# Row maxima of the mLSTM gates turned into columns: a masked sum on VectorE in place of sixteen one-row products on TensorE

## The chip, the cores and the metric

One core of a Trainium2 chip runs the whole kernel in one launch. The metric is device time in microseconds, from the first to the last instruction of the program as the device reports it; several runs are made and their median is given.

## What is computed

A trunk of two pre-norm residual layers over 256 frames of width 1024. Layer 0 mixes by pooling and forgetting attention and ends in a dense SwiGLU; layer 1 mixes by stick-breaking attention (8 heads of 64) and mLSTM (4 heads of 128) and ends in a top-2-of-8 expert SwiGLU. The change lies in the mLSTM of layer 1. Cut to that:

```python
log_i, log_f = gate_chunks(i_pre), log_sigmoid(gate_chunks(f_pre))
bcum = jnp.cumsum(log_f, axis=-1)
log_d = bcum[..., :, None] - bcum[..., None, :] + log_i[..., None, :]
m_out = jnp.maximum(inter, jnp.max(jnp.where(tri, log_d, -jnp.inf), axis=-1))
d_mat = jnp.exp(log_d - m_out[..., None])
num, den = ..., ...
h = num / jnp.maximum(jnp.abs(den), jnp.exp(-m_out))[..., None]
```

For each head and frame the kernel needs the running maximum in two layouts. As a row (frames along the free axis, the same row on all 128 partitions) it goes into the exponents of d_mat; as a column (frames along the partitions) it goes into exp(-m_out), the floor of the denominator.

## The kernel before

The matrices are multiplied as sums of three products of a high and a low part. A weight piece of 128x2048 lands in `raw` (six slots), ACT writes its high part (`make_high`, L674), DVE its low part (`make_low`, L679, "the subtraction"), and PE multiplies (L881 to L883). There are three buffers for the parts, so step n of the odd mixer splits piece n+3.

The odd mixer is a loop over 14 steps, `ODD_JOBS`, that each engine walks in its own program, in an order written out by hand. In step n PE first projects job n (`project`: 48 products, some 6 us), and then does the small products that the tables put into step n. The tables near the change are `SB_SCORES = {3: 0, 5: 2, 8: 4, 10: 6}` (scores of a pair of stick-breaking heads, L1210 and L1213), `SB_LATER = {4: 0, 6: 2, 9: 4, 11: 6}` (L1222 to L1224), `SB_VALUES = {5: 0, 7: 2, 10: 4, 12: 6}` (weights times values, L1003 and L1005), `ROWS_TURNED_AT = 8`, `SILU_AT = 9` and `ML_EXPONENTS_AT = 11`.

One pair of stick-breaking heads goes round the engines, here heads 4 and 5:

- PE writes scores at the end of step 8 (L1210, L1213); ACT takes abs, exp and log of them (L1678, L1679, L1682); DVE makes two parts per head (L2156, L2158); POOL masks the first part (L1849).
- At the end of step 9 PE sums it over later keys (L1222 to L1224); DVE subtracts that (L2168); ACT takes the exponential (L1688); POOL masks it (L1849); PE multiplies it with the values at the end of step 10 (L1003).

The row maxima are made in steps 2 and 3 (`gate_rows`, a scan on DVE) as `ml_r`, 128 x (4 heads x 256 frames), each row repeated on all partitions. In step 8, after its projection, PE turns them (`rows_to_columns`, L1197): 8 fp32 products of a 1x128 row with a 1x1 one, which the trace shows as 16 instructions, give 8 columns in bank 3, two tiles by four heads. DVE subtracts the column of sums from the bank (L2224) into `m_em`, at the end of its own step 8, behind the parts of heads 4 and 5 and a chunk of the convolution (L2139, L2142), and ahead of the subtraction of piece 11. ACT takes the exponential of `m_em` in step 11 (L1721); DVE reads it in step 12 (L2192). Bank 3 is next filled in step 9, by the sum of head 5 (L1222, the second of its pair).

Of the kernel before, what the change touches and what calls it, by code (L numbers as in the profile page):

```python
# [30 lines left out]
ALU = mybir.AluOpType  # L31
# [3 lines left out]
P = 128  # L35
# [10 lines left out]
ML_H = 4  # L46
# [229 lines left out]
def plan_banks():  # L276
    banks = Banks()

    def norm(j):
        for i in range(4):  # L280
            banks.fill(("norm", j, i), i)

    norm(0)
    banks.fill("vectors", 2)
    banks.fill("fgate_rows", 5)
    banks.fill("fgate", 4)
    for n in range(EVEN_STEPS):
        if n < len(EVEN_JOBS):
            banks.fill(("even", n), 6 + n % 2)
        if n == EVEN_SUMS_AFTER:  # L290
            banks.fill("frows", 3)
        if n in FOX_SCORES:
            for i in range(2):
                banks.fill(("fox_s", FOX_SCORES[n] + i), i)
        if n in FOX_TURNS:
            for i in range(2):
                banks.fill(("fox_pt", FOX_TURNS[n] + i), 2)
        if n in FOX_VALUES:
            banks.fill(("fox_o", FOX_VALUES[n] // 2), 3, 2)
        for g2 in range(2):  # L300
            if n == POOL_AT:
                banks.fill(("pool", g2), 4 + g2)
            if n == POOL_AT + 1:
                banks.fill(("poolmix", g2), 4 + g2)
    for t in range(T):
        for nh in range(2):
            banks.fill(("wout", 0, 2 * t + nh), 6 - 2 * t + nh)
    norm(1)
    for c in range(NCH):
        for j in range(4):  # L310
            banks.fill(("g", c, j), j % 2)
            banks.fill(("u", c, j), 2 + j % 2)
    for n in range(4):
        banks.fill(("fdown", n), 4 + n)
    norm(2)
    banks.fill("mgate_rows", 5)
    banks.fill("mgate", 4)
    for n in range(len(ODD_JOBS)):
        banks.fill(("odd", n), 6 + n % 2)
        if n == ODD_SUMS_AFTER:  # L320
            banks.fill("mcum", 2)
        if n in ODD_ROWS_AFTER:
            for h in ODD_ROWS_AFTER[n]:
                banks.fill(("mrow", h), 4 + h % 2)
        for i in range(2):
            if n in SB_SCORES:
                banks.fill(("sb_z", SB_SCORES[n] + i), i)
            if n in SB_LATER:
                banks.fill(("sb_lat", SB_LATER[n] + i), 2 + i)
        if n in SB_VALUES:  # L330
            banks.fill(("sb_o", SB_VALUES[n] // 2), 4 + SB_VALUES[n] // 2 % 2, 2)
        if n == ROWS_TURNED_AT:
            banks.fill("mr", 3)
        for i in range(2):
            if n in ML_SCORES:
                banks.fill(("ml_s", ML_SCORES[n] + i), i)
            if n in ML_VALUES:
                banks.fill(("ml_n", ML_VALUES[n] + i), 2 + i)
    for n in range(4):
        banks.fill(("wout", 1, n), 4 + n)  # L340
    for h in range(ML_H):
        banks.fill(("ml_t", h), h % 2)
    for t in range(T):
        for half in range(2):
            banks.fill(("xt", t, half), 2 * t + half)
    for t in range(T):
        banks.fill(("rparts", t), 5 - t, NQ)
    banks.fill("router", 6)
    banks.fill("rank", 5)
    banks.fill("counts", 7)  # L350
    for k in range(DK):
        banks.fill(("gather", 0, k), NG + k % NG)
    for k in range(DK):
        banks.fill(("gather", 1, k), 6 + k % 2)
    before = list(banks.count), list(banks.signals)
    banks.fill("sgt", 7)
    for part in range(len(PARTS)):
        for r in range(NG):
            banks.fill(("mg", part, r), r, NQ)
            banks.fill(("mu", part, r), NG + r, NQ)  # L360
    for r in range(NG):
        banks.fill(("md", r), DOWN_BANKS[r], NQ)
    for q in range(NQ):
        banks.fill(("mc", q), NG + q)
    per_item = [[a - b for a, b in zip(*pair)] for pair in zip((banks.count, banks.signals), before)]
    return banks.uses, *per_item


def build_trunk(nc, x_d, w, cst_d, out_d):
    uses, bank_fills_per_item, bank_signals_per_item = plan_banks()  # L370

    with ExitStack() as ctx:
# [3 lines left out]
        def sem(name):  # L376
            return ctx.enter_context(nc.semaphore(name))
# [12 lines left out]
        def ps(use):  # L390
            return bank[uses[use][0]][:, :]
# [198 lines left out]
        conv_silu = sem("conv_silu")  # L590
        mr_ready = sem("mr_ready")
        mem_ready = sem("mem_ready")
        sbl_ready = sem("sbl_ready")
        sbsp_ready = sem("sbsp_ready")
        sbsp_masked = sem("sbsp_masked")
# [263 lines left out]
        def _(pe):  # L859
# [328 lines left out]
                    last = mm(ps(use)[:, SEQ + t * P:SEQ + (t + 1) * P], li[t], ident, start=True, stop=True)  # L1188
                last.then_inc(fill_sem(use), 1)

            def rows_to_columns():

                open_bank(pe, "mr")
                pe.wait_ge(mr_ready, ML_H)
                for t in range(T):
                    for h in range(ML_H):
                        last = mm(ps("mr")[:, t * ML_H + h:t * ML_H + h + 1], ml_r[0:1, h, t * P:(t + 1) * P],  # L1197
                                  ones[0:1, 0:1], start=True, stop=True)
                last.then_inc(fill_sem("mr"), 1)

            def stick_scores(g):

                pair = (g, g + 1)
# [53 lines left out]
            for n in range(len(ODD_JOBS)):  # L1257
                if n:
                    project("odd", n, ODD_JOBS, N_ODD)
                else:  # L1260
                    first_odd_half(1)
                    small_columns("mgate", 2 * ML_H)
                if n == ODD_SUMS_AFTER:
                    pe.wait_ge(mlf_ready, 1)
                    prefix_sums("mcum", ml_lf, ML_H)
                for h in ODD_ROWS_AFTER.get(n, ()):
                    gate_rows(h)
                if n in SB_LATER:
                    for i in range(2):
                        stick_later(SB_LATER[n] + i)  # L1270
                if n == ROWS_TURNED_AT:
                    rows_to_columns()
                if n in SB_SCORES:
                    stick_scores(SB_SCORES[n])
                if n in SB_VALUES:
                    stick_values(SB_VALUES[n])
                for i in range(2):
                    if n in ML_VALUES:
                        ml_values(ML_VALUES[n] + i)
                    if n in ML_SCORES:  # L1280
                        ml_scores(ML_SCORES[n] + i)
# [222 lines left out]
        def _(act):  # L1504
# [193 lines left out]
            for n in range(len(ODD_JOBS)):  # L1698
                if n not in DVE_ODD_JOBS:
                    act.wait_ge(*filled(("odd", n)))  # L1700
                    dst, scale, shape = job_target(ODD_JOBS[n])
                    func = ACT.Sigmoid if ODD_JOBS[n][1] == "mo" else ACT.Copy
                    fn(dst, shape(ps(("odd", n))), func, scale=scale).then_inc(drain_sem(("odd", n)), 1)
                if n + 1 == min(SB_SCORES):
                    fn(unread[:, :], inv_ms[:, 2, :], ACT.Exp)
                if n in SB_SCORES:
                    stick_logs(SB_SCORES[n])
                if n in SB_VALUES:
                    mix_high_part(SB_VALUES[n] // 2, ("sb_o", SB_VALUES[n] // 2))
                high_parts(N_ODD + n + SPLITS)  # L1710
                if n in SB_LATER:
                    stick_weights(SB_LATER[n])
                if n == SILU_AT:

                    act.wait_ge(conv_ready, 8)
                    for half in range(2):
                        v = mqk[:, 4 * half:4 * half + 4, :]
                        fn(v, v, ACT.Silu).then_inc(conv_silu, 1)
                if n == ML_EXPONENTS_AT:
                    act.wait_ge(*drained("mr"))  # L1720
                    fn(m_em, m_em, ACT.Exp).then_inc(mem_ready, 1)  # L1721
                    for h in range(ML_H):
                        act.wait_ge(me_in, h + 1)
                        fn(ml_e[h], ml_e[h], ACT.Exp).then_inc(me_ready, 1)
                if n == len(ODD_JOBS) - 1:
                    fn(unread[:, :], inv_ms[:, 2, :], ACT.Sqrt)
                for i in range(2):
                    if n in ML_VALUES:
                        ml_squares(ML_VALUES[n] + i)
# [140 lines left out]
        def _(dve):  # L1870
# [328 lines left out]
            for n in range(len(ODD_JOBS)):  # L2199
# [20 lines left out]
                    if n in CONV_AT:  # L2220
                        conv_chunk(2 * CONV_AT[n] + 1)
                if n == ROWS_TURNED_AT:
                    dve.wait_ge(*filled("mr"))
                    V.tensor_tensor(m_em, ps("mr")[:, 0:T * ML_H].rearrange("p (t h) -> p t h", t=T), m_rn_f,  # L2224
                                    ALU.subtract).then_inc(drain_sem("mr"), 1)
                if n == ML_EXPONENTS_AT:
                    for h in range(ML_H):
                        ml_exponent(h)
# [293 lines left out]
```

## Time and profile before

| | |
|---|---|
| runs | 1427.05, 1425.03, 1422.69 us; median 1425.03 us |
| the profiled execution | span 1422.2 us; the page gives no other time for it |
| PE busy | 1394.8 us of 1422.2 (98%) |
| DVE, ACT, POOL busy | 441.0, 328.8 and 29.7 us |
| the odd mixer's steps 7 to 11 | from about 421 us to 461 us of the span |

The times are medians over whole executions; the profile is of one execution, and every time inside the kernel is counted from the start of its span. A row of a timeline gives the start, the length, the engine and the line; in brackets stands how long the engine had been idle before it and what released it. PEclk is the share of the full TensorE clock that was granted.

### The profile page before, as it was taken

The numbers are of one execution on the slowest core, as the hardware profiler recorded it, in microseconds if no ns is written. First come the engines' busy times: TensorE is split into PE (matmuls) and PEld (weight loads), VectorE is DVE, ScalarE is ACT, GpSimd is POOL, SyncE is SP. The second block draws the span as 40 slices with busy tenths as digits, with TensorE's granted clock in tenths as the row PEclk, the third lists the DMA queues.
The fourth block names the chain that finished last, engine by engine and source line by source line (L and its number), as shares of the span: only waits on it lengthen the run. The fifth ranks groups of instructions, "written<-read, shape, count | busy, mean of one in ns | idle before, by whom it ended". The sixth has DMA issues, their size and how long they took to land.

```text
span 1422.2 us, 33237 instructions
## 1 busy us (share of the span) xinstructions
PE 1394.8 (98%) x15137; PEld 833.4 (59%) x15137; DVE 441.0 (31%) x748; ACT 328.8 (23%) x528; POOL 29.7 (2%) x42
## 2 busy tenths in 40 slices
PE   6999999999999999999999999999999999999997
PEld 6987888888899853453453353353354354344344
DVE  4656655655686742101101101101101101101102
ACT  4645545445566531000000000000000000000001
POOL 2000000000012100000000000000000000000000
PEclk9999999999999999999999999999999999999998
DMA  9734555556443489999999999999999999999980
GB/s 296 252 119 146 195 177 194 191 180 198 149 120 140 148 332 326 401 419 389 391 418 387 392 417 389 394 415 393 388 414 400 392 405 402 393 402 408 393 332 32
DMA packets 133041, 438.42 MB, mean 308 GB/s; under 512 B 10690, under 2 KB 64160, under 8 KB 116512
## 3 DMA queue, kind: packets, MB, share of 16 engines
q1 hardware_dynamic: 131824, 433.26, 80.1%
q0 software_dynamic: 1072, 2.98, 0.7%
q8 instruction: 121, 1.98, 0.6%
q14 instruction: 24, 0.20, 0.0%
HBM read 435.16 MB, written 1.05 MB: 307 GB/s over the span
## 4 chain that ended last, share of the span: by engine, by line
PE 95%; DVE 3%; DMA 1%; issue 0%; ACT 0%; POOL 0%; SPq 0%; DVEq 0%
PE bank L1366 41%; PE bank L1387 20%; PE bank L1131 6%; PE bank L881 6%; PE bank L883 6%; PE bank L882 6%; PE bank L1132 4%; PE bank L1134 1%; PE bank L1415 1%; PE bank L1435 1%; DMA raw<-in_ev_w_in 1%; DVE arena L2142 0%; PE bank L1003 0%; PE bank L1049 0%; POOL arena L1849 0%
## 5 line engine op out<-in xcount | busy, mean ns | idle before, releaser
L1366 PE MATMUL bank<-ring,arena 128*32 128x512 f32 (+1 forms) x6144 | 583.5, 540 | 0.0
L1366 PEld LDWEIGHTS bank<-ring,arena 128*32 128x32 f32 x6144 | 197.7, 110 | 365.2 <-issue 362.5
L1387 PE MATMUL bank<-ring,arena 128*32 128x256 f32 x5376 | 291.5, 379 | 0.0
L1387 PEld LDWEIGHTS bank<-ring,arena 128*32 128x32 f32 x5376 | 175.1, 110 | 116.7 <-issue 3.1
L679 DVE TENSOR_TENSOR low<-raw,high 128x2048 fp32r<-128x2048 f32 x73 | 167.3, 2294 | 85.1 <-ACT high L674 84.9
L674 ACT ACTIVATE high<-raw 128x2048 fp32r<-128x2048 f32 x73 | 139.3, 1910 | 55.8 <-PE bank L883 44.1
L1131 PE MATMUL bank<-ht_both,high 128*128 128x512 f32 x392 | 140.5, 398 | 0.6 <-DVE ht_both L1901 0.6
L2413 DVE TENSOR_TENSOR expert_rows<-expert_rows,bank 128x512 f32<-128x512 f32 (+1 forms) x48 | 29.8, 621 | 344.3 <-issue 217.3
L1788 ACT ACTIVATE expert_rows<-bank 128x512 f32<-128x512 f32 (+1 forms) x48 | 25.9, 544 | 422.9 <-PE bank L1366 422.9
L1132 PE MATMUL bank<-ht_both,low 128*128 128x256 f32 x448 | 116.8, 281 | 0.0
L1799 ACT ACTIVATE y_h<-bank 128x256 fp32r<-128x256 f32 x24 | 9.2, 383 | 403.9 <-PE bank L1387 403.9
L2425 DVE TENSOR_TENSOR y_l<-bank,y_h 128x256 fp32r<-128x256 f32 x24 | 10.2, 425 | 270.5 <-ACT y_h L1799 270.5
L1132 PEld LDWEIGHTS bank<-ht_both,low 128*128 128x128 f32 x448 | 84.7, 189 | 5.1
L1131 PEld LDWEIGHTS bank<-ht_both,high 128*128 128x128 f32 x392 | 73.8, 188 | 16.1 <-issue 0.8
L881 PE MATMUL bank<-ht_both,high 128*128 128x256 f32 x224 | 65.9, 294 | 2.4 <-DVE ht_both L1901 1.8
L883 PE MATMUL bank<-ht_both,low 128*128 128x256 f32 x224 | 64.7, 289 | 0.0
L882 PE MATMUL bank<-ht_both,high 128*128 128x256 f32 x224 | 64.7, 289 | 0.0
L881 PE MATMUL bank<-high,ht_both 128*128 128x256 f32 x160 | 47.0, 294 | 0.1
L881 PEld LDWEIGHTS bank<-ht_both,high 128*128 128x128 f32 x224 | 44.2, 197 | 3.5 <-DVE ht_both L1901 2.2
L882 PE MATMUL bank<-low,ht_both 128*128 128x256 f32 x160 | 46.1, 288 | 0.0
L883 PE MATMUL bank<-high,ht_both 128*128 128x256 f32 x160 | 46.0, 288 | 0.0
L2259 DVE TENSOR_SCALAR sgt<-bank,cst 128x256 fp32r<-128x256 f32 x24 | 10.1, 478 | 113.5 <-PE bank L1399 113.5
(316 smaller groups left out, 1206.8 us busy)
## 6 DMA issues: line engine op xcount, KB each, us to landing
ring<-in_moe_w_down SPq DMA_DIRECT2D x112, 1024.0 KB, 8.4
ring<-in_moe_w_gate SPq DMA_DIRECT2D x64, 1024.0 KB, 9.1
ring<-in_moe_w_up SPq DMA_DIRECT2D x64, 1024.0 KB, 8.6
ring<-in_moe_w_gate SPq DMA_DIRECT2D x64, 768.0 KB, 5.9
ring<-in_moe_w_up SPq DMA_DIRECT2D x64, 768.0 KB, 6.6
raw<-in_ffn_w_gate SPq DMA_DIRECT2D x14, 1024.0 KB, 5.0
raw<-in_ffn_w_up SPq DMA_DIRECT2D x14, 1024.0 KB, 5.0
raw<-in_ffn_w_down SPq DMA_DIRECT2D x14, 1024.0 KB, 5.0
```

The lines of the kernel that those rows point to most:

```text
L674: nc.scalar.activation(high[:, n % SPLITS, :], raw[:, raw_slot(n), :], ACT.Copy).then_inc(high_ready, 1)
L679: nc.vector.tensor_tensor(low[:, n % SPLITS, :], raw[:, raw_slot(n), :], high[:, n % SPLITS, :].bitcast(F32), ALU.subtract).then_inc(split ...
L881: mm(out, l_high, r_high, start=start, stop=False)
L882: mm(out, l_high, r_low, start=False, stop=False)
L883: return mm(out, l_low, r_high, start=False, stop=stop)
L1131: mm(both, wh[:, k, cols], ht_pairs[:, :, k, :], start=k == 0, stop=False)
L1132: mm(both[:, 0, :], wl[:, k, cols], ht_h[:, k, :], start=False, stop=False)
L1134: last = mm(both, wh[:, k, cols], ht_pairs[:, :, k, :], start=False, stop=True)
L1366: ins = mm(ps(use)[q * GRP:(q + 1) * GRP, 0:width], rows[:, k, r * GRP:(r + 1) * GRP], weights[:, q, :, :], start=k == 0, stop=k == DK - 1)
L1387: ins = mm(ps(use)[q * GRP:(q + 1) * GRP, 0:DN], m_act_t[:, r, first + c, :], ring[:, at + c * DM + q * DN:at + c * DM + (q + 1) * DN], st ...
L1788: fn(m_silu[:, r, 0:WIDTHS[part]], ps(use)[:, 0:WIDTHS[part]], ACT.Silu).then_inc(drain_sem(use), 1)
L2413: V.tensor_tensor(m_act[:, r, 0:width], m_silu[:, r, 0:width], ps(use)[:, 0:width], ALU.mult).then_inc(drain_sem(use), 1)
```

## The change

The sixteen products and their bank are gone. In the same place of its program DVE multiplies the rows by the identity (`ident`, 128x128, repeated over heads and tiles) into the first 1024 columns of `hn`, which is free there, sums each block of 128 along the free axis, and subtracts the column of sums as before. ACT waits for a semaphore of its own in place of the bank's.

```diff
-        if n == ROWS_TURNED_AT:
-            banks.fill("mr", 3)
...
+        mem_set = sem("mem_set")
...
-            def rows_to_columns():
-
-                open_bank(pe, "mr")
-                pe.wait_ge(mr_ready, ML_H)
-                for t in range(T):
-                    for h in range(ML_H):
-                        last = mm(ps("mr")[:, t * ML_H + h:t * ML_H + h + 1], ml_r[0:1, h, t * P:(t + 1) * P],
-                                  ones[0:1, 0:1], start=True, stop=True)
-                last.then_inc(fill_sem("mr"), 1)
-
...
-                if n == ROWS_TURNED_AT:
-                    rows_to_columns()
...
-                    act.wait_ge(*drained("mr"))
+                    act.wait_ge(mem_set, 1)
                     fn(m_em, m_em, ACT.Exp).then_inc(mem_ready, 1)
...
                 if n == ROWS_TURNED_AT:
-                    dve.wait_ge(*filled("mr"))
-                    V.tensor_tensor(m_em, ps("mr")[:, 0:T * ML_H].rearrange("p (t h) -> p t h", t=T), m_rn_f,
-                                    ALU.subtract).then_inc(drain_sem("mr"), 1)
+                    rows = ml_r.rearrange("p h (t c) -> p h t c", t=T)
+                    marked = hn[:, 0, :].rearrange("p (h t c) -> p h t c", h=ML_H, t=T)
+                    steps.done(V.tensor_tensor(marked, rows, ident[:, None, None, :].to_broadcast([P, ML_H, T, P]),
+                                               ALU.mult))
+                    steps.done(V.tensor_reduce(m_em.rearrange("p t h -> p h t"), marked, AX, ALU.add))
+                    V.tensor_tensor(m_em, m_em, m_rn_f, ALU.subtract).then_inc(mem_set, 1)
```

DVE's own order at the end of step 8 and the start of step 9, before (`arena` holds the mixer's tiles, `s_cols` the small columns, `m_em` among them):

```order
L2142 SCALAR_TENSOR_TENSOR arena<-arena,vec 128x253 [waits dve_step]
L2224 TENSOR_TENSOR s_cols<-bank,s_cols 128x8 [waits filled3]
L679 TENSOR_TENSOR low<-raw,high 128x2048 [waits high_ready]
L2168 TENSOR_TENSOR arena<-arena,bank 128x384 [waits filled2,drained0]
L2168 TENSOR_TENSOR arena<-arena,bank 128x384 [waits filled3,drained1]
L679 TENSOR_TENSOR low<-raw,high 128x2048 [waits high_ready]
```

And now (lines from 679 on have moved up by one, those behind the removed function by 11 to 13):

```order
L2129 SCALAR_TENSOR_TENSOR arena<-arena,vec 128x253 [waits dve_step]
L2212 TENSOR_TENSOR hn<-arena,cst 128x1024
L2214 TENSOR_REDUCE s_cols<-hn 128x4x2 [waits dve_step]
L2215 TENSOR_TENSOR s_cols<-s_cols 128x8 [waits dve_step]
L678 TENSOR_TENSOR low<-raw,high 128x2048 [waits high_ready]
L2155 TENSOR_TENSOR arena<-arena,bank 128x384 [waits filled2,drained0]
L2155 TENSOR_TENSOR arena<-arena,bank 128x384 [waits filled3,drained1]
L678 TENSOR_TENSOR low<-raw,high 128x2048 [waits high_ready]
```

Two instructions of 1024 elements a partition now stand ahead of the subtraction of piece 11 and of the two L2168 (now L2155) of heads 4 and 5; the wait for bank 3's products is gone.

PE's order at the end of step 8, before:

```order
L883 MATMUL bank<-ht_both,low 128x256
L1197 MATMUL bank<-cst,arena 128x1 [waits mr_ready,drained3]
L1197 MATMUL bank<-cst,arena 128x1 x7
L1210 MATMUL bank<-arena 128x256 [waits drained0,drained1,drained6]
L1210 MATMUL bank<-arena 128x256
L1213 MATMUL bank<-arena 128x128 x2
```

And now:

```order
L882 MATMUL bank<-ht_both,low 128x256
L1199 MATMUL bank<-arena 128x256 [waits drained0,drained1,drained6]
L1199 MATMUL bank<-arena 128x256
L1202 MATMUL bank<-arena 128x128 x2
```

The scores of heads 4 and 5 follow the projection at once; each of these fp32 products is two instructions of the trace, so that the eight one-column products here are the sixteen of the profile.

## Rows read from the trace of the kernel before

**Rows 1.** The page, part 1 (busy us, share, instructions) and part 4 (chain, by engine).

```profile
PE 1394.8 (98%) x15137; PEld 833.4 (59%) x15137; DVE 441.0 (31%) x748; ACT 328.8 (23%) x528; POOL 29.7 (2%) x42
...
PE 95%; DVE 3%; DMA 1%; issue 0%; ACT 0%; POOL 0%; SPq 0%; DVEq 0%
```

**Rows 2.** Timeline of PE around the sixteen products: start us, us, engine, line, what.

```profile
435.45 1.94 PE L1197 MATMUL bank<-cst,arena 1*128 1x1 f32 x16
437.32 0.70 PE L1210 MATMUL bank<-arena 64*128 64x256 f32 x4
437.85 0.39 PE L1213 MATMUL bank<-arena 64*128 64x128 f32 x4
```

**Rows 3.** Windows of PE alone: length, busy us (x), PEclk, DMA share, GB/s.

```profile
432.00:444.00 12.00, 12.00 (x90) 0.86 0.28 87
```

**Rows 4.** Windows: length, busy us (x) of PE, PEld, DVE, ACT, POOL, PEclk, DMA.

```profile
438.00:439.00 1.00, 1.00 (x12) 0.88 (x9) 0.06 (x1) 0.70 (x2) 0.00 (x0) 0.90 0.70 287
439.00:440.00 1.00, 1.00 (x7) 1.00 (x7) 0.00 (x0) 0.94 (x3) 0.00 (x0) 0.50 0.02 8
...
441.00:442.00 1.00, 1.00 (x7) 1.00 (x6) 0.00 (x0) 0.99 (x2) 0.00 (x0) 0.50 0.00 0
442.00:443.00 1.00, 1.00 (x9) 1.00 (x9) 0.74 (x2) 1.00 (x3) 0.10 (x1) 0.90 0.00 0
```

**Rows 5.** Timeline of DVE, steps 7 to 9; in brackets idle time before, and releaser.

```profile
424.10 1.01 DVE L2168 TENSOR_TENSOR arena<-arena,bank 128x384 f32<-128x384 f32 x2
...
442.26 0.56 DVE L2156 SCALAR_TENSOR_TENSOR arena<-bank,arena 128x384 f32<-128x384 f32 x1 [4.20 <-ACT arena L1682]
...
446.21 0.16 DVE L2224 TENSOR_TENSOR s_cols<-bank,s_cols 128x8 f32<-128x8 f32 x1
...
448.48 1.01 DVE L2168 TENSOR_TENSOR arena<-arena,bank 128x384 f32<-128x384 f32 x2
449.41 2.28 DVE L679 TENSOR_TENSOR low<-raw,high 128x2048 fp32r<-128x2048 f32 x1
```

**Rows 6.** Groups of DVE by form: busy us, mean ns of one | idle before.

```profile
L693 DVE TENSOR_TENSOR low<-raw,high 128x1024 fp32r<-128x1024 f32 x2 | 2.4, 1220 | 1.2 <-ACT high L688 1.2
...
L2250 DVE TENSOR_TENSOR hn<-hn 128x512 f32<-128x512 f32 x2 | 1.4, 692 | 0.1
...
L2334 DVE TENSOR_REDUCE s_cols<-s_cols 128x16 f32<-128x128 f32 x1 | 0.3, 288 | 0.0
```

**Rows 7.** Timeline of POOL, steps 7 to 11.

```profile
425.29 3.35 POOL L1849 TENSOR_TENSOR arena<-arena,cst 128x256 f32<-128x256 f32 x2 [5.34 <-ACT arena L1688]
...
450.05 2.95 POOL L1849 TENSOR_TENSOR arena<-arena,cst 128x256 f32<-128x256 f32 x2 [5.46 <-ACT arena L1688]
460.11 0.74 POOL L1849 TENSOR_TENSOR arena<-arena,cst 128x256 f32<-128x256 f32 x1 [7.12 <-DVE arena L2156]
```

**Rows 8.** Timeline of ACT, steps 8 to 10.

```profile
438.27 0.49 ACT L1678 ACTIVATE arena<-bank 128x384 f32<-128x384 f32 x1 [6.45 <-PE bank L1213]
...
449.44 0.94 ACT L1688 ACTIVATE arena<-arena 128x384 f32<-128x384 f32 x2
...
451.69 2.00 ACT L1718 ACTIVATE arena<-arena 128x1024 f32<-128x1024 f32 x2
454.19 0.49 ACT L1678 ACTIVATE arena<-bank 128x384 f32<-128x384 f32 x1 [0.50 <-PE bank L1213]
```

**Rows 9.** Timeline of PE, the weights' products of steps 7, 10 and 11.

```profile
428.70 0.65 PE L1003 MATMUL bank<-arena 128*64 128x256 f32 x4 [0.99 <-POOL arena L1849]
...
454.09 0.65 PE L1003 MATMUL bank<-arena 128*64 128x256 f32 x4
...
460.99 0.67 PE L1222 MATMUL bank<-arena,cst 128*128 128x256 f32 x2
```

**Rows 10.** Timeline of PE in the norm ahead of the dense SwiGLU.

```profile
125.11 1.29 PE L871 MATMUL bank<-cst,hn 128*128 128x128 f32 x8 [1.53 <-DVE hn L1894]
```

**Rows 11.** Window of the same stretch.

```profile
124.00:126.00 2.00, 0.85 (x6) 0.67 (x7) 1.92 (x5) 0.74 (x3) 0.00 (x0) 1.00 0.00 0
```

## Prediction

> **What bounds the kernel now.** Read the busy times first, then the chain that ended last: TensorE (PE) is busy for 98% of the span and makes 95% of the chain [rows 1]. So a microsecond taken off PE counts, unless something else is ready only then. Next comes PE's timeline at the end of step 8: the sixteen one-row products start at 435.45, and the scores of heads 4 and 5 behind them at 437.32 and 437.85 [rows 2], so the products hold PE for 1.87 us.
>
> The third view is the granted clock, and it shows a second cost. Taken in windows of 12 us over the whole span, PEclk is 1.00 everywhere but at the start, in the last two windows, and in the one from 432, with 0.86 [rows 3]. In windows of one us that fall is from 438.8 to 442.2, at half the clock (1.2 of 2.4 GHz): 0.90 in the window from 438, 0.50 in the three from 439 to 442, 0.90 in the one from 442 [rows 4]. That makes 0.2 + 3 x 1 + 0.2 = 3.4 us at half, so at most 1.7 us of work is lost. What PE did ahead of it were the one-row products, and then scores of 64 rows [rows 2]. The scores without one-row products stand in three other steps, and there the clock didn't fall, so I take it that the fall goes with the products.
>
> Last come the timelines of DVE, POOL and ACT, and PE's own where it waits for them, at the weights of a pair of heads [rows 5, 7 to 9]: in step 7 L1003 stood idle 0.99 us for POOL's mask [rows 9].
>
> **The change, part by part.** Off PE go 1.87 us of products and up to 1.7 us by the half clock, 3.6 us together. That is the most this change can give.
>
> On DVE two instructions come in and the small subtraction stays. The product of 128x1024 costs 1.22 us by the nearest row, L693, also a two-operand fp32 instruction of 1024 elements [rows 6]. For the sum no row has this size: 128 elements into 16 sums took 288 ns, and a product of 512 elements 692 ns [rows 6]. From 288 to 692 for 384 elements more is 1.05 ns an element, and 1024 elements come to 692 + 512 x 1.05 = 1.23 us. I take 2.45 us for both and leave the few hundredths between them out. The bounds: both at the price of half the length, 2 x 0.69 = 1.4 us; or the sum paid anew for each of its eight blocks, 8 x 0.288 = 2.3 us [rows 6], 3.5 us with the product.
>
> Now the place. DVE waits 4.20 us in step 8 for ACT's logs of heads 4 and 5 [rows 5], and ACT had waited 6.45 us for their scores [rows 8]. Both have room, so this chain comes 1.87 us earlier with PE (it hangs on the scores, ahead of the half clock): DVE reaches L2224's place at 446.21 - 1.87 = 444.34. From L2224 to the two L2168 of step 9 it took 448.48 - 446.21 = 2.27 us, the subtraction of piece 11 between them [rows 5]. That stays, with 2.45 us ahead of it: L2168 starts at 444.34 + 2.45 + 2.27 = 449.06, **0.6 us later than before although PE is earlier.** The removed wait for the products had cost DVE nothing, since they ended 9 us ahead of L2224 [rows 2, 5]. PE's next fill of bank 3 no longer waits for L2224; no idle stands in the trace there, so I price that at nothing.
>
> Behind L2168 queue ACT's exponential, POOL's masks and PE's L1003. Step 7 shows that chain where DVE sets it: L2168 starts at 424.10, the two masks run from 425.29 to 428.64, 4.54 us after it, and L1003 follows at 428.70 [rows 5, 7, 9]. In step 9 ACT came last, and the masks ended at 453.00 [rows 7], 1.1 us ahead of L1003 at 454.09 [rows 9]. That 1.1 us is all the cover there was. Now the masks end at 449.06 + 4.54 = 453.60. PE, 3.6 us earlier, is there at 450.5, so it **waits some 3.1 us** and starts L1003 at about 453.65: of 3.6 us, 0.4 are left.
>
> The two masks are long there (2.95 us, against 0.74 for one in step 10 [rows 7]) while DVE's subtraction of piece 12 runs beside them, from 449.41 for 2.28 us [rows 5]. The Trainium skill, page "SBUF — State Buffer", section "Who interferes with whom", has it that a DVE instruction with two SBUF inputs contends with a GpSimd one that reads SBUF. By that the new product, with both inputs in SBUF, could hold up the masks of step 8 as well. They start from L2156, though, 3.95 us ahead of L2224's place [rows 5], and two of 0.74 fit in between, so the sum stays.
>
> What is late next is ACT in step 10. Before, its exponentials ended at 450.38, a table load and two Silu followed up to 453.69, and it idled 0.50 us until the scores of heads 6 and 7 at 454.19 [rows 8]. Now the second L2168 ends at 449.06 + 1.01 = 450.07 and its exponential, half of 0.94, at about 450.6, 0.2 later; Silu ends at 453.9, and ACT goes on at once, 0.3 us earlier than before. DVE's parts and POOL's mask follow it to PE's L1222 of step 11, which at 460.99 is just behind the mask that ran from 460.11 for 0.74 us [rows 7, 9]. PE would be there 0.4 us earlier, the mask 0.3. So 0.3 us come out of the odd mixer, and the experts' stage behind it passes them on.
>
> The subtractions of pieces 11 and 12 end 0.6 us later, and their slots are free for the next loads that much later. No DMA is added or moved, and DMA makes 1% of the chain [rows 1]; I price that at nothing. Were a first load of the experts just in time, it would cost those 0.6 us.
>
> **The sum.** The profiled execution's span is 1422.2 us, and the page gives no other time for it; the median of the runs is 1425.03, 2.8 us above. The change takes 0.3 us off: 1421.9 against the span and **1424.7 us** against the median.
>
> **Rivals.**
>
> 1. *The wait doesn't bind.* If masks and ACT kept pace, PE's 3.6 us would come through: 1425.0 - 3.6 = 1421.4. For it: PE is 95% of the chain. Against it: only 1.1 us of cover stood ahead of L1003, and ACT had 0.50 us. In part it happens if the two instructions are cheaper, since the chain over DVE and ACT moves one for one with their price: at the bound of 1.4 us the gain is 0.3 + 1.05 = 1.4 us, and at 3.5 us the change loses 0.8. It turns at 2.75 us.
>
> 2. *The new wait costs the clock* (the other side). PE would stand idle some 3 us in step 10 between products with 64 rows (L1210, L1213) and with 64 columns (L1003). Before, 1.87 us of one-row products between full work and 64-row products were followed by 3.4 us at half [rows 2, 4]. If the same follows here, up to 1.7 us of work is lost behind the wait, less the 0.4 that PE has: 1.3 us slower, 1426.3. It decides as soon as half clock behind the wait costs over 0.4 us. Against it: in the norm PE stood 1.53 us at one place, and had 0.85 busy us in 2, at full clock [rows 10, 11]; but nothing in the middle of this trace is an idle stretch of 3 us, and I give the rival two thirds of the forecast's chance. The Trainium skill, page "TensorE: Matmul & The Clock Gate", section "Why this matters for your kernels", warns of throughput drops in the middle of a kernel from idle gaps between bursts of matmuls. By that rule this rival is the likelier, and the time 1426.3.
>
> 3. *The fall of the clock isn't the products'.* Then PE is 1.87 us earlier in place of 3.6, which still reaches the wait at 452.2, and the time is the forecast's, 1424.7.
>
> **How the numbers follow.** About 0.3% (4.3 us) is what a measurement of this kernel can tell from no change. Forecast 0.45, rival 1 with its partial forms 0.15, rival 2 0.30, rival 3 0.05, and 0.05 for what I don't see. All the named cases lie between 1421.4 and 1426.3, inside 4.3 us of the median on both sides; only the scatter of the runs (1422.69 to 1427.05, some 2 us to each side) added to an outer case can go beyond. So no change has 0.91, faster 0.05 (rival 1 is nearest to its bound), slower 0.04. The range takes rival 1 at its full price below, and above it rival 2 with 1.5 us of scatter: 1421.4 to 1427.8.
>
> **What would show it.** Right: in the changed profile DVE's two new instructions take about 1.2 us each; no half clock behind step 8's projection; L1003 of step 10 idle some 3 us for POOL; L1222 of step 11 at about the old time. Rival 1 shows as no idle at L1003, rival 2 as a stretch at 0.50 behind it. Wrong: the odd mixer's end moves by over 2 us, or the experts' stage, untouched here, changes its own length by more than the mixer.

## The result, and the profile of the changed kernel

The changed kernel takes 1427.10 us (median of 12 runs, 1423.17 to 1430.10), the kernel before, measured beside it, 1424.35 us (12 runs, 1422.69 to 1427.05). The ratio is 1.0019 with an interval of 1.0011 to 1.0026: **slower by 2.7 us, from 1.6 to 3.7**. The forecast was 1424.7, slightly faster; the time lies in its range (1421.4 to 1427.8), on rival 2's side. It is within the 0.3% that the forecast called no change, but twelve runs a side tell it from nothing.

In the page's parts 1 and 4 PE has 16 instructions less and still makes nearly the whole chain, 93% now [rows 1]:

```profile
PE 1394.4 (98%) x15121; PEld 830.6 (58%) x15121; DVE 443.1 (31%) x750; ACT 329.2 (23%) x528; POOL 30.1 (2%) x42
...
PE 93%; DVE 3%; DMA 1%; issue 1%; ACT 1%; SPq 0%; POOL 0%; DVEq 0%
```

The two executions differ at the start: before's stood at half clock from 15 to 23 us, this one didn't. So all times below are counted from step 7's weights, 428.70 before [rows 9] and 427.54 now, where PE waited for POOL 0.99 us in both. PE's timeline, steps 7 to 11:

```profile
427.54 0.65 PE L1002 MATMUL bank<-arena 128*64 128x256 f32 x4 [0.99 <-POOL arena L1836]
...
435.18 0.70 PE L1199 MATMUL bank<-arena 64*128 64x256 f32 x4 [0.83 <-DVE arena L1919]
...
450.02 0.39 PE L1202 MATMUL bank<-arena 64*128 64x128 f32 x4
453.41 0.65 PE L1002 MATMUL bank<-arena 128*64 128x256 f32 x4 [3.00 <-DVE arena L1919]
...
461.57 0.60 PE L1211 MATMUL bank<-arena,cst 128*128 128x256 f32 x2
```

Two waits are new. In step 8 the scores of heads 4 and 5 (L1199) waited 0.83 us for DVE, where the products had stood [rows 2]. In step 10 the weights (L1002) waited 3.00 us. From step 7, L1002 of step 10 is at 25.87 us (25.39 before), L1211 of step 11 at 34.03 (32.29 before [rows 9]): 0.48 us late ahead of the products of steps 10 and 11, 1.74 behind them. DVE's timeline shows what the first waits for, and what makes the chain behind the second late:

```profile
434.38 0.69 DVE L1919 TENSOR_SCALAR arena<-bank 128x512 f32<-128x512 f32 x1 [1.23 <-PE bank L882]
...
444.03 1.22 DVE L2212 TENSOR_TENSOR hn<-arena,cst 128x1024 f32<-128x1024 f32 x1
445.28 1.22 DVE L2214 TENSOR_REDUCE s_cols<-hn 128x8 f32<-128x1024 f32 x1
446.54 0.17 DVE L2215 TENSOR_TENSOR s_cols<-s_cols 128x8 f32<-128x8 f32 x1
446.62 2.29 DVE L678 TENSOR_TENSOR low<-raw,high 128x2048 fp32r<-128x2048 f32 x1
448.82 1.01 DVE L2155 TENSOR_TENSOR arena<-arena,bank 128x384 f32<-128x384 f32 x2
449.75 2.29 DVE L678 TENSOR_TENSOR low<-raw,high 128x2048 fp32r<-128x2048 f32 x1
```

L1919 at 434.38 is the drain of job 8, which the scores of heads 4 and 5 read (`SB_ROWS_FROM = {0: (1, 2), 4: (6, 8)}`). In the kernel before it stood in the same place, under PE's one-row products of 435.45 to 437.32:

```profile
435.56 0.69 DVE L1932 TENSOR_SCALAR arena<-bank 128x512 f32<-128x512 f32 x1 [1.24 <-PE bank L883]
```

Behind the sum, ACT's exponential and POOL's masks of heads 4 and 5 are late (timelines of ACT and of POOL; [rows 7, 8]):

```profile
449.40 0.99 ACT L1675 ACTIVATE arena<-arena 128x384 f32<-128x384 f32 x2 [3.53 <-DVE arena L2155]
```

```profile
450.01 3.30 POOL L1836 TENSOR_TENSOR arena<-arena,cst 128x256 f32<-128x256 f32 x2 [7.60 <-ACT arena L1675]
```

ACT waits for DVE now, which it did not before, and the masks end at 453.31, 0.10 us ahead of L1002. The bracket puts PE's 3.00 us down to DVE's L1919, but that ended at 452.64 in step 10; what came last was POOL. The granted clock moved too (windows of PE and the other engines: length, busy us of each, PEclk, DMA share, GB/s; [rows 4]):

```profile
440.00:441.00 1.00, 1.00 (x11) 1.00 (x10) 0.90 (x2) 1.00 (x3) 0.26 (x1) 1.00 0.00 0
...
454.00:455.00 1.00, 1.00 (x10) 0.83 (x7) 0.00 (x0) 0.98 (x2) 0.00 (x0) 0.66 0.86 352
455.00:456.00 1.00, 1.00 (x6) 1.00 (x6) 0.00 (x0) 0.96 (x3) 0.00 (x0) 0.50 1.00 426
456.00:457.00 1.00, 1.00 (x6) 1.00 (x6) 0.00 (x0) 0.97 (x2) 0.00 (x0) 0.50 0.28 115
457.00:458.00 1.00, 1.00 (x8) 1.00 (x7) 0.00 (x0) 0.98 (x2) 0.00 (x0) 0.64 0.00 0
```

Behind step 8 the clock is full; behind the wait it is at half (1.2 of 2.4 GHz) for 3.4 us. From L1002 to L1211 PE needs 8.16 us, 6.90 before: the fall costs some 1.26 us. The router's first transposes start at 503.86 against 503.40, counted from step 7 1.62 us late. There the changed kernel's execution falls again, and before's didn't (windows of PE over the router's stage and the first gathers, the changed kernel, then the kernel before):

```profile
505.00:525.00 20.00, 18.24 (x135) 0.83 1.01 408
```

```profile
505.00:525.00 20.00, 18.24 (x157) 1.00 0.99 410
```

From the router's start to the end of the span (1425.5 and 1422.2 us) the changed kernel takes 921.6 us here, the kernel before 918.8: the fall in the router's stage costs 2.8 us in this pair.

### The profile page after: what moved, and what is told of

It reads as the page before. It is cut to its first block, busy times and chain, and to the rows that moved or that the text cites. A ratio compares the mean times of both kernels' runs of the same rounds, so it can differ in the third digit from the quotient of the medians.

```text
span 1425.5 us, 33206 instructions
## 1 busy us (share of the span) xinstructions
PE 1394.4 (98%) x15121; PEld 830.6 (58%) x15121; DVE 443.1 (31%) x750; ACT 329.2 (23%) x528; POOL 30.1 (2%) x42
## 3 DMA queue, kind: packets, MB, share of 16 engines
q8 instruction: 121, 1.98, 0.6%
## 4 chain that ended last, share of the span: by engine, by line
PE 93%; DVE 3%; DMA 1%; issue 1%; ACT 1%; SPq 0%; POOL 0%; DVEq 0%
PE bank L1353 41%; PE bank L1374 20%; PE bank L1130 6%; PE bank L880 5%; PE bank L882 5%; PE bank L881 5%; PE bank L1131 4%; DMA raw<-in_ev_w_in 1%; PE bank L1402 1%; PE bank L1133 1%; PE bank L1422 1%; DVE arena L2129 1%; DVE low L678 0%; PE bank L1002 0%; PE bank L1048 0%
```

## The experiments

**Theory A:** the sum's place in DVE's program, ahead of heads 4 and 5's subtraction, makes PE wait 3 us in step 10, and the clock falls behind the wait. The rivals: the two instructions cost their 2.4 us wherever they stand; the removed products matter; the clock has no share; or the router's stage, later only by the change, is where the time goes.

**The sum two steps later on DVE.** The same block of code, put behind the drain at a step's start and run in step 10, so behind both L2155 and the drain of job 10; ACT needs the result in step 11.

```diff
-ROWS_TURNED_AT = 8
+ROWS_TURNED_AT = 10
...
+                if n == ROWS_TURNED_AT:
+                    rows = ml_r.rearrange("p h (t c) -> p h t c", t=T)
...
-                if n == ROWS_TURNED_AT:
-                    rows = ml_r.rearrange("p h (t c) -> p h t c", t=T)
...
```

> The changed kernel with the masked sum moved on DVE from the end of step 8 to step 10, behind the drain of job 10, where DVE waits some 6 us for ACT. Theory A (the place costs: the sum stands ahead of the exponents' subtraction of heads 4 and 5, PE then waits 3 us for POOL and loses the clock): that subtraction comes 2.6 us earlier than in the changed kernel, PE waits at most 0.6 us in step 10, no half clock follows it, PE reaches step 11's prefix sums some 2 us earlier than before (counted from step 7), and the time is about 1422.2 us, ratio to before 0.998 to 0.999. Theory B (the place doesn't matter: the sum's reads and writes, or a later stage, cost the 2.7 us): the time stays at 1.0015 to 1.002.

Measured: 1422.80 us (11 runs), 0.9985 of the kernel before (0.9975 to 0.9996): faster than both. PE's timeline, then DVE's:

```profile
437.75 0.70 PE L1199 MATMUL bank<-arena 64*128 64x256 f32 x4 [0.83 <-DVE arena L1919]
...
453.39 0.65 PE L1002 MATMUL bank<-arena 128*64 128x256 f32 x4 [0.40 <-issue]
...
460.38 0.67 PE L1211 MATMUL bank<-arena,cst 128*128 128x256 f32 x2 [0.17 <-POOL arena L1836]
```

```profile
448.80 1.01 DVE L2155 TENSOR_TENSOR arena<-arena,bank 128x384 f32<-128x384 f32 x2
...
452.78 1.59 DVE L2195 TENSOR_TENSOR hn<-arena,cst 128x1024 f32<-128x1024 f32 x1
454.41 1.22 DVE L2197 TENSOR_REDUCE s_cols<-hn 128x8 f32<-128x1024 f32 x1
```

The 0.83 us stay, the 3 us are 0.40 (POOL's masks end at 453.29), no half clock follows in the mixer, and L1002 is at 23.29 us from step 7 (430.10) in place of 25.87. L1211 of step 11 is at 30.28, 2.0 us earlier than before's 32.29, and there PE waits for POOL's next mask. So the place is what costs, not the instructions, nor that the products are gone: they are gone here too.

**Products and sum both.** The kernel before with the two new instructions ahead of L2224, which overwrites their result.

> The kernel before, sixteen products kept, with the two added DVE instructions (product with the identity and sum) ahead of its subtraction in step 8; their result is overwritten by the subtraction from the products. Theory A: the subtraction of heads 4 and 5 in step 9 starts 2.5 us later than before, the masks end near 455.5 on the clock of the profile before, PE waits 1.4 us in step 10 at full clock or with a fall behind it, and the time is 1.4 to 2.8 us above before, ratio 1.001 to 1.002. Theory B' (removing the products is what costs, since they covered a wait): as before, ratio 1.000.

Measured: 1429.61 us, 1.0032 (1.0022 to 1.0043). Slower, but by 4.6 us in place of the expected 1.4 to 2.8, and by another wait (PE's timeline):

```profile
450.08 1.22 PE L1222 MATMUL bank<-arena,cst 128*128 128x256 f32 x2 [2.37 <-DVE s_cols L2229]
...
459.23 0.65 PE L1003 MATMUL bank<-arena 128*64 128x256 f32 x4
```

The drain of the products' bank had moved behind the two instructions, and step 9's sum of head 5 fills that bank. So this run does not test the wait in step 10. Half clock stands behind the products, as before [rows 4], and again behind this wait (windows of PE):

```profile
440.00:441.00 1.00, 1.00 (x7) 0.50 0.02 8
...
451.00:452.00 1.00, 1.00 (x6) 0.50 0.08 16
```

**The wait filled.** The changed kernel, with 26 products of 128x128x256 into unread columns of the bank that step 10 fills next, ahead of L1002's wait.

```diff
+                if n == FILL_AT:
+                    open_bank(pe, ("sb_o", SB_VALUES[n] // 2))
+                    for _ in range(FILL):
+                        mm(ps(("sb_o", SB_VALUES[n] // 2))[:, SEQ:2 * SEQ], ht_h[:, 0, 0:P], ht_h[:, 1, :], start=True,
+                           stop=True)
```

> The changed kernel with 26 full products (128x128 by 256 columns, 0.12 us each, 3.1 us) on PE ahead of step 10's weights-by-values products, into columns of the bank that nothing reads. If the half clock behind the wait is part of the loss: the weights-by-values products start where they did in the changed kernel, the clock stays full in step 11, and the time is some 1.3 us below the changed kernel, ratio to before about 1.0010. If the wait alone is the loss and the half clock is hidden by ACT and POOL behind it: as the changed kernel, 1.0019.

Measured: 1424.59 us, 1.0000 (0.9990 to 1.0010). PE's timeline, and a window behind the wait:

```profile
450.24 3.37 PE L1267 MATMUL bank<-ht_both 128*128 128x256 f32 x26
453.54 0.65 PE L1004 MATMUL bank<-arena 128*64 128x256 f32 x4
```

```profile
455.00:456.00 1.00, 1.00 (x11) 1.00 0.99 418
```

The values start as late as in the changed kernel (26.11 us from step 7, at 427.43), yet the time is 2.5 us less. With PE at work in the wait the clock holds, so the clock has a share of its own. In this execution the router's stage held as well, which may be why the 2.5 us are more than the mixer's 1.26.

**How regular are the falls?** Two more executions of each kernel.

> A second look at the kernel before. Theory A (one-row products count as idle TensorE for its clock): a stretch of some 3.4 us at half clock begins within 3 us of the end of the sixteen products in step 8, as in the first profile. Rival (the fall's place is chance, whatever PE does): it stands elsewhere or not at all. A fall in the router's stage (behind 505 us) may or may not be there; it doesn't hang on the change.

> A third look at the kernel before, expectations as for the second: a fall behind step 8's products by theory A, none or elsewhere by the rival.

> A second look at the changed kernel. Theory A: PE waits about 3.0 us in step 10 and a stretch at half clock of some 3.4 us begins within 3 us of that wait's end, or in it; none stands behind step 8. Rival (chance): full clock there in this execution. A fall in the router's stage may or may not be there.

> A third look at the changed kernel, expectations as for the second: a fall behind step 10's wait by theory A, none there by the rival.

Before took 1424.19 and 1424.03 us, the changed kernel 1425.92 and 1427.18. In all three traces of before the clock falls behind the products and holds in the router's stage; in all three of the changed one it falls behind step 10's wait and again in the router's stage. A fall at the start, 15 to 23 us, stands in all three of before and one of the changed kernel. That is ahead of the change, so it isn't the change's. From step 7 to the router's start the three traces of before take 74.7 us and those of the changed kernel 76.3; from there to the end of the span 918.8 us, against 921.6, 920.3 and 920.3. (Why the one-row products bring a fall is not shown by any run; what the expectation says of it is a guess.)

**The router's stage kept busy.** Nine identity products in place of seven ahead of the rank, and two into unread columns ahead of each of the first gather's two waits, in the kernel before, in the changed one and in the one with the sum in step 10.

```diff
-            for _ in range(7):
+            for _ in range(9):
...
+                    if (half, k) == (0, 0):
+                        open_bank(pe, ("gather", 0, 1))
+                        for _ in range(2):
+                            mm(ps(("gather", 0, 1))[:, GATHERED:GATHERED + P], ident, u_inc, start=True, stop=True)
```

> The kernel before, with TensorE kept busier in the router's stage: nine identity products in place of seven ahead of the rank, and two 128x128 fp32 products into columns that nobody reads ahead of each of the two waits of the first gather. The three traces of before show no half clock in that stage. Both theories: 1424 us, within 0.3% of before, and no half clock at 500 to 530 us. If runs of before near 1426.8 us come from a fall of the clock in that stage (theory B), such runs are missing here and the median is near 1423.

> The changed kernel with the same products in the router's stage. Theory A: the mixer's loss stays (PE waits 3.0 us in step 10, half clock for some 3 us behind it, the router starts 1.5 us later than in before), the fall at 513 to 519 us is gone, 1425.5 to 1426, that is 1.5 to 1.8 us over the kernel before with the same products instead of 2.7. Theory B: the fall in the router's stage stays, the difference stays at 2.7 us.

> The masked sum in step 10 of VectorE's program (as in the run that moved it there, 1422.8 us) with the same products in the router's stage. Theory A (the sum's place on VectorE is the loss in the mixer, and the fall in the router's stage is a second loss that these products take away): no half clock from 436 to 530 us, 1420.5 to 1422, 1.5 to 2 us under the kernel before with the same products. Theory B (the router's fall has nothing to do with TensorE's idle time there): the half clock of 511.8 to 515.0 stays, 1422.8.

Measured, each with 11 runs: before 1422.85 (0.9988, 0.9979 to 0.9997), changed 1425.55 (1.0005, 0.9996 to 1.0014), sum in step 10 1420.83 (0.9974, 0.9965 to 0.9982). The stage stands at full clock in all three; in the changed kernel (windows of PE):

```profile
125.00:133.00 8.00, 7.15 (x28) 0.57 0.21 68
456.00:461.00 5.00, 5.00 (x31) 0.66 0.50 190
505.00:525.00 20.00, 19.64 (x164) 1.00 0.88 357
```

Each lost 1.5 to 2.0 us against itself without these products, before too: its runs end at 1425.28 here, at 1427.02 without the products. I take it that some of its executions have the router's fall, although the three traces don't show it. But the difference that I had put to the router's stage did not shrink as theory A said: 2.4 us by the ratios (1.0005 over 0.9988), 2.7 by the medians. The executions still scattered over up to 4 us here, and the first row shows another fall that can do that: in the second norm, far ahead of the change.

**The sum one step later.** `ROWS_TURNED_AT = 9`, without other edits: behind both L2155 of heads 4 and 5, ahead of the drain of job 10.

> The changed kernel with the masked sum one step later in VectorE's program, so behind the subtraction for heads 4 and 5 and ahead of the drain of job 10, which the values of step 10 need. Theory A (what counts is which of TensorE's waits is last behind the two instructions): the masks of POOL end 2.4 us earlier than in the changed kernel, but the drain of job 10 comes 2.4 us later; TensorE waits some 2.2 us in step 10, for VectorE in place of POOL, the clock may fall behind it (0.5 to 1.3 us), and the time is between the sum in step 10 (1422.8) and the changed kernel (1427.1): 1423.5 to 1426. Rival (the two instructions cost their 2.4 us wherever they stand): 1427.

Measured: 1425.19 us, 1.0004 (0.9993 to 1.0014). PE's timeline, and a window of PE behind it:

```profile
452.74 0.65 PE L1002 MATMUL bank<-arena 128*64 128x256 f32 x4 [2.28 <-DVE arena L1919]
```

```profile
454.00:458.00 4.00, 4.00 (x23) 0.57 0.54 225
```

Now POOL's masks are ready at 449.72 and DVE's drain of job 10 is last, as expected, and the clock falls behind 2.28 us too. There are two things late in turn, and only behind the second is DVE free.

**All the other stages kept busy.** The three kernels with the router's products, and besides 8 identity products ahead of the first projection's wait, and 9 and 4 ahead of the second norm's two halves, into columns that are written again; the fourth is the changed kernel with these and the 26 products in step 10's wait.

```diff
+                        if (j, i) == (1, 0):
+                            for _ in range(4 if t else 9):
+                                mm(ps(("norm", j, 0))[:, P:2 * P], ident, ident, start=True, stop=True)
...
+                        if use == ("even", 0) and c == k == 0:
+                            for _ in range(8):
+                                mm(ps(use)[:, SEQ:SEQ + P], ident, ident, start=True, stop=True)
```

> The kernel before with the router's products and, besides, TensorE kept at work in the waits of the first two norms (8, 9 and 4 identity products into columns that are written again), where the half clock of 15 to 23 or 125 to 133 us (3.4 us of clock) stands in ten of the thirteen traces. Expected: only the half clock behind the one-row products stays; most of the spread goes; 1422 to 1422.6.

> The changed kernel with the same products. Theory A (the difference is the mixer's alone: PE's wait in step 10 and the half clock behind it): 1.6 us over the kernel before with the same products, from 1.3 to 1.9. Rival (the router's and the norms' stages had a share in the 2.7 us, or there is a further loss that no trace has shown): 2.4 or more, or 1 or less.

> The changed kernel with the same products and the 26 products in step 10's wait. Theory A: the clock's share goes (1.26 us), the delay of the masks stays: 0.3 to 0.5 us over the kernel before with the same products. Rival (the clock has no share in the mixer's loss): 1.6 over.

> The masked sum in step 10 of VectorE's program with the same products. Theory A: no half clock anywhere, 2.0 us under the kernel before with the same products, that is near 1420.3. Rival (the earlier gain was the other stages' clock): less than 1 us under it.

(The early falls stand in nine of the thirteen traces, not in ten as written there.) Measured:

| all other stages kept busy | median, us | against before so filled | router's start in the trace, from step 7 |
|---|---|---|---|
| before | 1422.86 | | 74.69 |
| changed | 1424.44 | +1.58 | 76.32 (+1.63) |
| changed, wait filled too | 1423.38 | +0.52 | 75.27 (+0.58) |
| sum in step 10 | 1420.88 | -1.98 | 72.68 (-2.01) |

The scatter is smaller (before 1422.63 to 1423.88; the changed kernel 1423.29 to 1425.73; the last one 1420.80 to 1421.00). Two runs of the changed kernel lie where those with the wait filled do, so its fall in the mixer may stay out now and then, and three at 1425.6 must hold a further loss; no trace shows either. Medians and traces agree, and the three differences come out as theory A says, within 0.02 us; before itself lies above its expected 1422 to 1422.6. With eleven runs a side the medians alone are less sure than that: drawn anew from the runs, the first difference has an interval of 1.4 to 2.7 us, the second of 0.3 to 0.7, the third of -2.2 to -1.8. The windows of PE behind step 10's wait, changed kernel and then with the wait filled:

```profile
453.00:459.00 6.00, 5.60 (x35) 0.72 0.51 191
```

```profile
453.00:459.00 6.00, 6.00 (x52) 1.00 0.54 185
```

So **the change's own cost is 1.6 us, by the medians and the traces together: 0.5 by late masks, 1.1 by the clock.** The split is good to some 0.2 us, since the 26 products themselves ran past the masks: the values start at 26.10 us from step 7 with them, at 25.88 without. The trace of before so filled holds one thing more. In that execution the clock did not fall behind the products (windows of PE, then its timeline):

```profile
436.00:444.00 8.00, 7.89 (x64) 1.00 0.20 78
```

```profile
434.26 1.94 PE L1203 MATMUL bank<-cst,arena 1*128 1x1 f32 x16
...
442.85 0.60 PE L1228 MATMUL bank<-arena,cst 128*128 128x256 f32 x2
...
445.22 0.70 PE L1228 MATMUL bank<-arena,cst 128*128 128x256 f32 x2 [1.33 <-DVE s_cols L2234]
...
452.89 0.65 PE L1009 MATMUL bank<-arena 128*64 128x256 f32 x4
```

PE reached step 9's sum earlier and waited 1.33 us there for the drain of the products' bank. From step 7 (427.52) its step 10 is at 25.37 us, against 25.39 with the fall. Behind the products the half clock had only stretched PE's work over a wait.

The quickest versions are the sum in step 10 with the router's products, 1420.83 us, and with all of them, 1420.88 (0.9979, 0.9970 to 0.9988): some 3.5 us under the kernel before.

## Why the prediction was wrong

**Right: the prices.** The product took 1.22 us and the sum 1.22, predicted 1.22 and 1.23; the small subtraction 0.17.

**Right: the wait and its place; its size by luck.** PE waited 3.00 us at L1002 of step 10 for POOL's masks, predicted 3.1. But both ends of the wait came about a microsecond later than forecast: PE was there at 22.87 us from step 7 in place of 21.8, and the masks ended at 25.77 in place of 24.90.

**Wrong: "this chain comes 1.87 us earlier with PE".** The scores follow PE's projection only if DVE's drain of job 8 is done; the products had hidden it. PE waited 0.83 us, and 1.0 us reached the chain. So L2155 came at 21.28 us from step 7, 0.92 later than the forecast's 20.36, and L1002 of step 10 at 25.87 in place of 24.95. This alone turns the gain of 0.44 us that the forecast saw at L1002 into a loss of 0.48 there, about the 0.5 us that was measured with the wait filled. The trace of before had the row: the drain from 435.56 to 436.25, beside the products and ahead of the scores' start.

**Wrong: the choice of forecast over rival 2.** The prediction gave "the new wait costs the clock" a chance of 0.30. It is what happened: half clock for 3.4 us right behind the 3.00 us, priced at up to 1.7, measured at some 1.26 in the first pair of traces and at 1.1 by filling the wait. The forecast put the clock behind the wait at nothing. The norm's 1.53 us at full clock [rows 10, 11] was held against the rival, but that place fell in five of the thirteen traces (125 to 133 us), so it was no sign of safety, only one execution. The Trainium skill, page "TensorE: Matmul & The Clock Gate", section "Why this matters for your kernels", which warns of idle gaps between bursts of matmuls, had made rival 2 the likelier; the traces agree with it at 3.00 us, and the wait of 2.28 us in the step-9 run did the same. That the time still lies in the range is owed to the 1.5 us of scatter that the range added to this rival's 1426.3.

**Right, but worth less than it looked: the fall goes with the products.** No trace without them has it at 438.8, and five of the six with them have it. The prediction's "3.6 us, the most this change can give" counted it as lost work; the filled kernel before shows that without the fall PE waits 1.33 us for the bank instead. That wait goes with the bank, so the changed PE does arrive earlier at step 10's scores (21.95 us from step 7 against 24.54, that is 2.6: the 3.6 less 0.83 and some).

**ACT's 0.3 us** did not show in the changed kernel: behind the fall POOL's next masks (from 459.51 and 460.44) had ended by 461.19, and PE came to L1211 at 461.57 by its own work. Where no fall stands that chain does bind: with the sum in step 10 PE waited 0.17 us there for POOL.

**Rival 3** was wrong, **rival 1** has its gain only when the sum stands where nobody waits for DVE: -2.0 us, not -3.6, since the drain's 0.83 us, 0.40 for the masks and 0.17 at L1211 come off it, and some 0.2 besides.

**The rest of the 2.7 us**, some 1.1, is not shown to be the change's. Falls at the start, in the second norm and in the router's stage come and go in these kernels, and with PE kept busy there the difference is 1.6, the lower end of the first interval. In the router's stage a fall costs 1.5 or 2.8 us by the traces: it is what made the experts' stage longer by more than the mixer in the first pair, a sign of being wrong that the prediction had named. Three traces of three have it against none of three before. A later start does not explain that: the trace of the sum in step 10 has it too, and there the router starts 2.0 us earlier than before. How much oftener it comes was not counted, and stays open.

## What to carry to other kernels

When work leaves the bottleneck engine, ask of the next instruction on it which drain or mask the removed work had been hiding, and look for that row beside it in the trace. Work moved to an engine with room still stands in a queue: put it behind what the bottleneck waits for next (here two steps later, 3.6 us apart from the worst place), and if a wait on TensorE remains, products that nobody reads can keep its clock. With a clock that falls in some executions, fill the thin places elsewhere before measuring an effect of one or two microseconds: here the runs of the sum in step 10 lay within 4.3 us (1420.58 to 1424.89) and then within 0.2.

## What was not expected of the hardware

- A half clock that cost nothing: 1.7 us of clock lost behind the products, and step 10 at 25.39 us against 25.37 without it.
- The falls are of two sizes. Summed over its windows of one microsecond, each fall in these traces, but for the last some ten us of the kernel, took 1.7 us (438.8, 454, most of those in the router's stage) or 3.4 us (15 to 23, 125 to 133, once 512 to 520) of full clock.
- The DVE product of 1.22 us took 1.59 in step 10, where it started at 452.78 beside POOL's mask that ran to 453.29. The Trainium skill, page "SBUF — State Buffer", section "Who interferes with whom", names this pair; the row agrees, and it cost nothing there.
